# Two groups of a feed-forward's down projection as Strassen's seven products, with x kept in DRAM meanwhile

## What is computed

```python
        hn = rmsnorm(h, norm_mlp_w[i])
        h = h + jnp.square(jax.nn.relu(hn @ w_ff1[i])) @ w_ff2[i]          # 1024 -> 4096 -> 1024
...
        h2 = rmsnorm_2(x, norm_ffn_g[i])
        up = jnp.einsum('bsd,df->bsf', h2, w_up[i])                        # 1024 -> 2 * 2816
        up = causal_depthwise_conv_2(up, conv_w[i], conv_b[i])
        act = jax.nn.gelu(up[..., :D_FF_2]) * up[..., D_FF_2:]
        x = x + jnp.einsum('bsf,fd->bsd', act, w_down[i])                  # 2816 -> 1024
        h3 = rmsnorm_2(x, norm_ple_g[i])
```

## Time and profile before

| what | us |
|---|---|
| device time, median of 3 runs | 1626.25 (1626.19 to 1626.27) |
| profiled execution, first to last instruction (the span) | 1624.8 |
| TensorE busy | 1606.2 (99%) |
| VectorE busy | 1027.4 (63%) |
| ScalarE busy | 695.8 (43%) |
| DMA, mean over the span | 108 GB/s |

### The profile page before, as it was taken

How to read it: one execution, slowest core, us unless ns; L and a number is a source line. 1 busy time by engine, 2 the same in 40 slices (tenths; PEclk the granted TensorE clock), 3 DMA queues, 4 the chain that set the end, 5 groups by cost and what they waited for, 6 DMA issues and landing times.

```text
span 1624.8 us, 19202 instructions
## 1 busy us (share of the span) xinstructions
PE 1606.2 (99%) x7616; PEld 1326.7 (82%) x7616; DVE 1027.4 (63%) x1455; ACT 695.8 (43%) x1016; POOL 174.4 (11%) x255
## 2 busy tenths in 40 slices
PE   9999999999999999999999999999999999999998
PEld 7878777888888888887788887888888888888888
DVE  6755788668384865657744578445567636736757
ACT  6524475535252524414662155442344314414544
POOL 0001145100000000014500255000000000000000
PEclk9999999999999999999999999999999999999999
DMA  5224231264757422331122211322322222222331
GB/s 189 80 88 138 87 128 53 78 207 129 233 130 233 129 104 82 126 130 54 51 104 78 96 60 53 134 100 104 104 91 104 104 93 89 104 104 86 120 107 52
DMA packets 30584, 176.17 MB, mean 108 GB/s; under 512 B 4064, under 2 KB 6560, under 8 KB 11040
## 3 DMA queue, kind: packets, MB, share of 16 engines
q1 hardware_dynamic: 24048, 151.81, 26.0%
q0 software_dynamic: 1728, 12.58, 4.1%
q10 hardware_dynamic: 4720, 10.56, 1.9%
HBM read 170.72 MB, written 4.23 MB: 108 GB/s over the span
## 4 chain that ended last, share of the span: by engine, by line
PE 89%; DVE 5%; issue 2%; ACT 2%; POOL 1%; DMA 1%; SPq 0%; DVEq 0%; POOLq 0%
PE bank L719 21%; PE bank L721 21%; PE bank L720 21%; PE bank L727 3%; PE bank L729 3%; PE bank L728 3%; PE bank L1109 2%; PE bank L1107 2%; PE bank L1108 2%; PE bank L920 1%; PE bank L905 1%; PE bank L1025 1%; DMA x<-in_x_t 1%; DVE q_blk L1991 0%; DVE k_blk L1991 0%
## 5 line engine op out<-in xcount | busy, mean ns | idle before, releaser
L719 PE MATMUL bank<-a_hi,w_hi 128*128 128x512 f32 x1184 | 465.5, 393 | 1.4 <-DVE w_lo L2073 0.7
L721 PE MATMUL bank<-a_hi,w_lo 128*128 128x512 f32 x1184 | 461.2, 390 | 0.0
L720 PE MATMUL bank<-a_lo,w_hi 128*128 128x512 f32 x1184 | 460.9, 389 | 0.0
L1291 ACT ACTIVATE w_hi<-w_raw 128x2048 fp32r<-128x2048 f32 x105 | 200.3, 1907 | 220.7 <-DMA w_raw<-in_strips 217.3
L1854 DVE TENSOR_TENSOR w_lo<-w_raw,w_hi 128x2048 fp32r<-128x2048 f32 x102 | 233.5, 2290 | 50.5 <-ACT w_hi L1291 50.4
L719 PEld LDWEIGHTS bank<-a_hi,w_hi 128*128 128x128 f32 x1184 | 222.4, 188 | 47.3 <-issue 1.5
L721 PEld LDWEIGHTS bank<-a_hi,w_lo 128*128 128x128 f32 x1184 | 222.2, 188 | 46.9
L720 PEld LDWEIGHTS bank<-a_lo,w_hi 128*128 128x128 f32 x1184 | 222.4, 188 | 44.1 <-issue 0.2
L719 PE MATMUL bank<-b_hi,w_hi 128*128 128x512 f32 x368 | 143.4, 390 | 0.4 <-DVE b_lo L2570 0.4
L720 PE MATMUL bank<-b_lo,w_hi 128*128 128x512 f32 x368 | 143.2, 389 | 0.0
L721 PE MATMUL bank<-b_hi,w_lo 128*128 128x512 f32 x368 | 143.2, 389 | 0.0
(11 more groups left out here) (362 smaller groups left out, 2571.6 us busy)
## 6 DMA issues: line engine op xcount, KB each, us to landing
w_raw<-in_strips SPq DMA_DIRECT2D x117, 1024.0 KB, 4.8
a_part<-in_parts SPq DMA_DIRECT2D x15, 1024.0 KB, 8.6
a_part<-in_parts POOLq DMA_DIRECT2D x12, 1024.0 KB, 9.8
seg_in<-cum_kept ACTq DMA_DIRECT2D x16, 256.0 KB, 3.7
spare<-in_parts SPq DMA_DIRECT2D x3, 1024.0 KB, 14.6
spare<-in_strips SPq DMA_DIRECT2D x3, 1024.0 KB, 4.9
x<-in_x_t SPq DMA_DIRECT2D x4, 512.0 KB, 7.1
head_bias<-in_rel ACTq DMA_DIRECT2D x1, 2048.0 KB, 11.7
```

Of the source, the lines that this page charges most:

```text
L719: mm(ps[:, :], w_hi[slot][:, k, cols], hi[:, k, :], start=(k == 0), stop=False)
L720: mm(ps[:, :], w_hi[slot][:, k, cols], lo[:, k, :], start=False, stop=False)
L721: return mm(ps[:, :], w_lo[slot][:, k, cols], hi[:, k, :], start=False, stop=(k == kt - 1))
L1291: run(w_hi[j], w_raw[j], ACT.Copy).then_inc(hi_split, 1)
```

## The change

`down0` and `down1` become the fourth and fifth group by seven products, a second series with sums of its own (`SERIES`, `added[1]`). Their combined sums are turned and added to x in phase `up2`: all at tiles 8 and 10 (`UP_TURNS`). For the room, x is stored to DRAM (`x_kept`) before the first of them and loaded again in `up2`; stages 0 and 1 of the weights' sums lie in its place. The activation goes to `hid` rather than to `b_hi` and `b_lo` in `up0` and `up1`. A fourth T buffer takes every third place in the new series.

In all five groups `a_difference` now writes in place, over quarter (0,0) in stage 2. So product 3's source is loaded a second time: SP waits until product 0 is done and then loads quarter (0,0) to the raw slot. The order of ScalarE's and VectorE's steps from product 2 on changes as well, in all five groups.

```diff
-SEVEN = [f"ff2_{g}" for g in range(FF_GROUPS - 1)]
+SEVEN = [f"ff2_{g}" for g in range(FF_GROUPS - 1)] + ["down0", "down1"]
+FF_SEVEN = FF_GROUPS - 1
...
-PHASES += [("up0", 8), ("down0", 4), ("up1", 8), ("down1", 4), ("up2", 6), ("down2", 4), ("ple", 1), ("gate", 4)]
+PHASES += [("up0", 8), ("down0", 7), ("up1", 8), ("down1", 7), ("up2", 6), ("down2", 4), ("ple", 1), ("gate", 4)]
...
+        PART_AT = [[work + 6144 + SW * j for j in range(3)], [place["x"], place["x"] + SW, work + 13344]]
...
             def other_parts(g):
...
+
+                sp_eng.wait_ge(unit_done, 2 * FIRST[SEVEN[g]] + 2)
+                sp_eng.dma_start(flat(strip_source(g, 3)), part_of((0, 0), g)).then_inc(part_loaded[2], 16)
                 sp_eng.wait_ge(strip_split, FIRST[SEVEN[g]] + 5)
...
+                if s == FIRST["up2"] + 3:
+
+                    sp_eng.wait_ge(strip_split, FIRST["down1"] + 7)
+                    sp_eng.dma_start(x, x_kept).then_inc(x_loaded[0], 16)
...
+            UP_TURNS = {(8, 1): 0, (8, 3): 1, (8, 5): 2, (8, 7): 3, (10, 1): 4, (10, 3): 5, (10, 5): 6, (10, 7): 7}
...
+            stream("up0", feature_k, A, ready=wait_tiles(NORMS["ffn2"]["lo"]), after=lambda j: direct_sums("ffn2") if j == 0 else None)
+            seven(FF_SEVEN)
+            stream("up1", feature_k, A)
+            seven(FF_SEVEN + 1)
+            stream("up2", feature_k, A, within=within_up2)
...
-                for step, i in ((t_high, 2), (a_high, 2), (a_high, 3), (t_high, 3), (a_high, 4), (t_high, 4), (a_high, 5), (t_high, 5),
-                                (a_high, 6), (t_high, 6)):
+                for step, i in ((a_high, 2), (t_high, 2), (t_high, 3), (a_high, 3), (a_high, 4), (t_high, 4), (a_high, 5), (t_high, 5),
+                                (a_high, 6), (t_high, 6)):
...
+            act.wait_ge(NORMS["ffn2"]["lo"], KT)
+            act.wait_ge(NORMS["ffn2"]["sq"], KT)
+            act.dma_start(x_kept, x).then_inc(spilled, 16)
...
+                    if by_seven and f in (9, 11):
+                        t_high(FF_SEVEN + g, f // 2 - 4)
+                    if by_seven and f in (12, 14):
+                        a_high(FF_SEVEN + g, f // 2 - 6)
...
-                v.tensor_tensor(w_raw[s % W_SLOTS], a_part[2], spare, ALU.subtract).then_inc(a_sum, 1)
+                v.tensor_tensor(both, both, spare, ALU.subtract).then_inc(a_sum, 1)
...
-                for step, i in ((t_low, 2), (a_low, 2), (t_sums, 3), (add_product, 0), (a_low, 3), (t_low, 3), (t_sums, 4), (add_product, 1),
-                                (a_low, 4), (t_low, 4), (a_low, 5), (t_low, 5), (t_sums, 6), (add_product, 3), (a_low, 6), (t_low, 6),
-                                (add_product, 4)):
+                for step, i in ((t_sums, 2), (a_low, 2), (t_low, 2), (t_sums, 3), (add_product, 0), (t_low, 3), (a_low, 3), (t_sums, 4),
+                                (add_product, 1), (a_low, 4), (t_low, 4), (a_low, 5), (t_low, 5), (t_sums, 6), (add_product, 3), (a_low, 6),
+                                (t_low, 6), (add_product, 4)):
...
+                    if by_seven:
+                        if f == 10:
+                            t_sums(n, 1)
+                            t_low(n, 0)
+                        if f == 12:
+                            t_low(n, 1)
+                            a_difference(n)
+                        if f in (13, 14):
+                            a_low(n, f - 13)
+                    else:
+                        down_sums(f)
...
+            def down_sums(f):
+
+                if f == 0:
+                    dve.wait_ge(dve_evac, EVAC0["up2"])
+                    c_pair(1, 0, ALU.add, 1)
+                    c_pair(1, 3, ALU.subtract, 1)
+                if f == 2:
+                    c_kept(1, 2, 1)
+                    c_pair(0, 4, ALU.add, 1)
+                if f == 4:
+                    c_pair(3, 5, ALU.add, 1)
+                    c_pair(5, 4, ALU.subtract, 1)
+                if f == 6:
+                    c_kept(5, 2, 1)
+                    c_kept(5, 6, 1)
+                if f in (8, 10):
+                    dve.wait_ge(x_loaded[0], 64)
+                    for m in range(2 * f - 16, 2 * f - 12):
+                        add_turned(m, 1)
```

More of the change, by code:

```diff
@@ L50 @@
 PHASES = [("xbc", 6), ("qk", 4), ("z", 4), ("v", 2), ("wo_ssd", 4), ("wo_att", 2)]
-SEVEN = [f"ff2_{g}" for g in range(FF_GROUPS - 1)]
+SEVEN = [f"ff2_{g}" for g in range(FF_GROUPS - 1)] + ["down0", "down1"]
+FF_SEVEN = FF_GROUPS - 1
+PRE = [f"ff1_{g}" for g in range(FF_SEVEN)] + ["up0", "up1"]
+NEXT = [f"ff1_{g + 1}" for g in range(FF_SEVEN)] + ["up1", "up2"]
+SERIES = [0] * FF_SEVEN + [1, 1]
+SERIES_FIRST, SERIES_LAST = {0, FF_SEVEN}, {FF_SEVEN - 1, FF_SEVEN + 1}
 T_PARTS = [((0, 0), None, 0), ((1, 0), (0, 0), -1), ((0, 0), (1, 1), -1), ((1, 0), (1, 1), -1), ((0, 1), (0, 0), -1), ((1, 1), None, 0),
@@ L460, in build, with t_slot, t_slot_free, strip_source @@
         SP_END = SP_A + SP_LOG
[L462 to L468, removed]
+        def t_slot(q):
+            return 3 if SERIES[q // 7] and q % 3 == 2 else q % 3
+        def t_slot_free(q):
+            first = 7 * FF_SEVEN if SERIES[q // 7] else 0
+            if q - 3 < first:
+                return 2 * FIRST[PRE[q // 7]]
+            return 2 * (FIRST[SEVEN[(q - 3) // 7]] + (q - 3) % 7) + 2
+        def strip_source(g, i):
+            stage = a_part[SERIES[g]]
+            return stage[A_STAGE[i]] if i in A_STAGE else {2: stage[2], 3: w_raw[(FIRST[SEVEN[g]] + 3) % W_SLOTS], 4: spare}[i]
+        def plain_count(g, i):
+            return PART0[2] + 16 * (2 * g + i - 1)
+        def hid_ready(g, n):
+            return (up_act, KT * (g - FF_SEVEN) + n) if SERIES[g] else (hid_done, HID0 + KT * g + n)
         def hid_half(part):
@@ L670, in _, with part_sums @@
             attention("1", "qk")
-            for g in range(len(SEVEN)):
+            def part_sums(g):
                 for i in A_STAGE:
@@ L687, in _ @@
             attention("2b", "qk2b")
+            for g in range(FF_SEVEN, len(SEVEN)):
+                part_sums(g)
             pool.wait_ge(x_scaled_out, POOL_OUT)
@@ L1100, in seven @@
                         if i in KEPT:
-                            ps, first, end = bank[KEPT[i] + t], g == 0, g == len(SEVEN) - 1
+                            ps, first, end = bank[KEPT[i] + t], g in SERIES_FIRST, g in SERIES_LAST
                         else:
@@ L2395, in last_group @@
                         lo(FIRST[phase] + m // 2 + 2)
-            for g in range(len(SEVEN)):
+            for g in range(FF_SEVEN):
                 seven_group(g)
@@ new lines, in down_last @@
+            def down_last():
+                lo(FIRST["up2"] + UP_TILES % KT + 1)
+                for k in range(2):
+                    dve.wait_ge(p_hi_ready, k + 1)
+                    v.tensor_tensor(p_lo[:, k, :], p_raw[:, k, :], p_hi[:, k, :].bitcast(F32), ALU.subtract).then_inc(p_lo_ready, 1)
+                for m in range(KT):
+                    dve.wait_ge(c_added, C_ADDED0 + KT + m + 1)
+                    add_x("down2", m, m)
+                    if m % 2 and m < KT - 1:
+                        lo(FIRST["down2"] + m // 2 + 2)
+                    low("ple", m, gains[:, 6, :], (a_hi, a_lo))
+                    add_square("ple", m)
+                    if m == KT - 1:
+                        lo(FIRST["down2"] + m // 2 + 2)
@@ L2737 @@
         "strips": np.concatenate(strips),
-        "parts": np.concatenate([by_half(ff2[j * D:(j + 1) * D]) for j in range(len(SEVEN))]),
+        "parts": np.concatenate([by_half(w[j * D:(j + 1) * D]) for w, n in ((ff2, FF_SEVEN), (down, 2)) for j in range(n)]),
         "gains": np.stack([by_tile(v) for v in gains], axis=1),
```

250 lines of the change are left out of this document (127 added, 123 removed).

## The result

The changed kernel takes 1631.5 us, median of 7 runs (1630.28 to 1633.2), against 1626.27 for the kernel before (7 runs). The ratio is 1.0033, with a 95% interval of 1.0024 to 1.0042: slower by 0.33%, or 5.2 us. The forecast was 1626.1. The second rival's price was 1631.6, within 0.1 us of what was measured.

The account below looks back on a forecast made before the run. TensorE, busy 1606.2 of 1624.8 us, was taken as the bound. Terms: -10.2 + 3.9 + 3.2 + 3.0 = -0.1 us, so 1626.25 - 0.1 = 1626.1 us, range 1620.5 to 1631.5.

Parts of the forecast that it names:

- second rival: Reload takes its neighbour's 8.6 us in all five groups: 2.35 us a group in `ff2`, 2.3 after; 1631.6 us, chance 0.19.
- turning and adding in `up2`: The 32 transposes go into `up2` and lengthen it by 3.9 us; the first transpose doesn't wait.
- waits in `down0`, `down1`: Late VectorE and ScalarE steps delay products 2, 3, 4 by 0.5, 0.9, 0.2 us: 3.2 us for both stages.
- waits in three `ff2` groups: Product 3 waits for its reloaded source in `ff2_0` to `ff2_2`: 1.0 us a group, 3.0 in all.
- X: Landing of product 3's reload, counted from the start of `ff2_0`: taken as 12.95 us, 13.2 if last to finish.
- X - 11.95: Wait of an `ff2` group in us, if positive, set by product 4, due at 21.95.
- the prediction's signs: If right: in `ff2_0` to `ff2_2` about 0.8 us wait before product 3, for `w_lo`, behind `w_hi` and a 7 us DMA.
- 40% of the engines: Share of DMA engines a load beside an accumulation got in the trace: 1 MB in about 6.5 us, alone 2.6.
- even shares: DMA engines alternating evenly between queues would land the reload at about 12.7, three `ff2` waits 2.3 us; not adopted.
- Fewer matmuls: `down0` and `down1` lose 24 matmuls each, 43.52 to 38.41 us: 10.2 us less.
- first rival: Reload is in time, no `ff2` group waits: 1623.1 us, down to 1619.9 with no waits at all; chance 0.27.
- x to DRAM and back: 2 MB each way, loaded again in `up2` in some 8 to 10 us, wanted about 40 us later: costs nothing.

Follow-up runs that it names:

- second profile: The changed kernel itself run and profiled again, nothing altered: 1631.52 us (5 runs), ratio 1.0033; the profiled execution took 1631.12 us.

## Why the prediction was wrong

By its own terms, in us:

| term | forecast | first profile | second profile |
|---|---|---|---|
| two stages at 38.41 instead of 43.52 | -10.2 | -10.2 | -10.2 |
| turning and adding in `up2` | +3.9 | +3.8 | +3.8 |
| waits in `down0`, `down1` | +3.2 | +3.5 | +3.4 |
| waits in three `ff2` groups | +3.0 | +9.9 | +7.5 |
| sum | -0.1 | +7.0 | +4.5 |
| growth of the span | | +6.7 | +4.6 |

(38.41 is taken from both `down` stages, and 115.40 from the three `ff2` stages. The first profile's 9.9 hold 2.9 us of the clock's fall. In the second profile `down0` and `down1` last 40.16 and 40.09 us, and `up2` 69.07.)

**The step that failed is the landing of the reload**, "I take 12.95", with its bound 13.2. Measured were X of 14.4 in `ff2_0`, and 14.6 and 13.8 in the two others (X - 11.95 = 2.4, 2.7 and 1.85). The mechanism, the place and the formula that turns X into a wait were right: the wait stands where TensorE needs `w_lo` for product 3, behind `w_hi` and the DMA, as the prediction's signs had it. Its size was wrong because X was. The bound of 13.2 came of adding up the data left to move, with all DMA engines busy to the end, and a lag of 0.7. The engines were busy, but the data ended at 14.0, 14.1 and 13.4, not at 12.5. For 3.5 to 3.9 us after its issue the reload moved nothing, where a lone load begins after 1.0; that is 2.5 to 3.0 us of the 3.3 to 4.3 by which it outlasted one. The rest is its slower transfer, with the late packets at the end. Neither the prediction's 40% of the engines nor even shares describe this: at first the reload had none. The lag was 0.3 to 0.5 us, an error the other way. And the sum was called the late end, though another row, the neighbour's 8.6 us, gave 14.3 and was left to a rival with 0.19. (That neighbour, too, was placed 0.3 us late: it was issued at 0.3 and landed at 8.9, not at 0.6 and 9.2.)

The experiments settle that the landing is the cause: with the load of stage 1 put behind the reload, or with product 5's accumulation cut, it lands in time and the waits are gone. How much of the lateness is the load's and how much the accumulation's stays open, and so does what keeps the reload's first packet back.

**The second rival** gave the time, 1631.6, though not in every part. In `ff2_0` to `ff2_2` it was nearly right (2.4, 2.7 and 1.8 us by the landings, for 2.35 each). In the second series it forecast 2.3 a stage; there the reload landed after 6.7 and 7.5 us and added nothing to 1.7 a stage. Its waits come to 11.6 us in all. The profile without a fall of the clock has 10.9 (7.5 and 3.4), and between span and device time lie 1.7 us where 1.4 were taken. That its price fits to 0.1 us is in part chance.

**Fewer matmuls** and **turning** are right: `up2` grew by 3.8 us for 3.9, and the run with the reload ahead has the time of the first rival, 1623.4 for 1623.1. **The waits of `down0` and `down1`** are right in size and in place: in `down0` the gaps on TensorE before products 2, 3 and 4, each with the slower first step behind it, cost 0.7, 0.7 and 0.2 us where 0.5, 0.9 and 0.2 were forecast, and moving one step of ScalarE took 1.4 us of the 1.7 a stage away. **x to DRAM and back**, costed at nothing, and the combination in `up2` cost nothing: `up2` has TensorE busy for 69.06 of 69.06 us, though VectorE has 54.84.

**The fall of the clock** was no term and no rival. It cost 1.4 to 1.5 us twice in the first profile and nothing in the second. The Trainium skill (TensorE: Matmul & The Clock Gate, section HAM oscillation) tells of a kernel whose waits for a DMA, longer than these, bring the clock down each time; here it came down after 2 of 6 waits of this kind in the two profiles.

## What to carry to other kernels

When a transfer gets a new deadline, put it ahead of those with later ones on its queue: that one move is worth 8.1 us here, and turns a loss of 5.2 us into a gain of 2.8. Bound the landing of a transfer in traffic by the slowest comparable transfer seen in such traffic, not by the data left to move: a transfer issued into traffic may begin late. And where a change touches a helper that several stages share, cost it first in the stages that are not the subject: a microsecond there counts once for each of them.

## What was not expected of the hardware

- A transfer's time to landing hangs on what its neighbours have left to do. 1 MB lands after 4.7 us alone, after 4.8 to 6.1 with no load ahead (in one case for its first 0.6 us) and an accumulating DMA that is near its end or has not yet begun to move data, and after 7.8 to 9.4 with another MB just ahead and 6 to 7 us of the accumulation to come (`ff2_0` to `ff2_2` of every profile with the reload behind the load). In `down0` and `down1`, where the accumulation landed 2.5 and 3.2 us after the reload was issued, it took 6.7 and 7.5.
- Most of that is a late start. With the accumulation in full course, the load issued into it moved its first packet 3.5 to 4.0 us after its issue (15 of 15 reloads, in five profiles), alone after 1.0. A load that had begun before the accumulation's data went on beside them, slower. The accumulation, too, moves its first packet 1.6 us after its issue with no load beside it (reload ahead), and after 4.1 to 4.8 with the load of stage 1 issued 0.3 to 0.4 us behind it (changed kernel).
- The reload landed 0.3 to 0.5 us after its last packet, as the lone load did. The load of stage 1, whose data end in the middle of the accumulation, took 0.9 to 1.2 us for the same in the kernel before.
- TensorE's granted clock fell to 1.2 GHz after idle times of 2.07, 2.2 and 2.45 us (from start to start, less a matmul's 0.23) and stayed at 2.4 GHz after others of 2.21, 2.69 and 2.83: the same kernel with nearly the same waits has it in one execution and not in the next.
